# Raw residual rows with their reciprocal root in the gathers of an expert layer, and an earlier request for the tenth weight piece

## The chip, the cores and the metric

The kernel runs on one core of a Trainium2 chip. The metric is the device time of one execution of the whole program in microseconds (us), the median of several runs.

## The reference

One inference step of a two-layer decoder, for a prompt of 256 tokens and 32 sample tokens (8 sequences of 4), 1024 wide, all in float32. Layer 0 is a gated DeltaNet mixer, layer 1 differential attention; each is followed by a mixture of experts, and it is this part that the change touches:

```python
h = h + hier_moe(rms_norm(h, norm_m[layer]), w_rg, b_rg, w_re, b_re, w_gate, w_up, w_down)

# rms_norm: x * rsqrt(mean(x*x) + EPS) * g
# hier_moe: softmax over 4 groups, the best group; softmax over its 8 experts, the best two
def expert_block(args):            # 32 experts, 1024 -> 512 -> 1024
    xblk, e = args
    hid = jax.nn.silu(xblk @ w_gate[e]) * (xblk @ w_up[e])
    return hid @ w_down[e]
```

Each token's output is the sum of its two experts' outputs, weighted by the gates. The root-mean-square factor of a token is one number for its row, so (r x) W = r (x W).

## The kernel before

The program runs five phases one after the other: `gdn_phase`, `moe_phase` for layer 0, `attn_phase`, `moe_phase` for layer 1, `final_phase`. Each phase is one block with an instruction stream for each engine, and semaphores order them by hand. SP issues the loads and stores.

**Expert weights.** All 32 experts' weights pass through SBUF once in a layer: 96 pieces of 2 MiB (gate, up and down of each expert). They go round through ten slots (`SLOT_COUNT`, `slots`). A group is two experts, so six pieces, and there are 16 groups, 0 to 15 (`LAST`). Pieces 0 to 8 are requested before the phase, or at its start (4 and 5 in layer 1). Piece 9 goes to the tenth slot (L2082). From piece 10 on a piece is requested when the one ten before it has been read: `load` (L2085) works in halves of 1 MiB and waits for `half_used` and `used`, `load_whole` (L2097) waits for `used`; TensorE raises both in `stage` and `products`. Everything goes through SP's one queue in order.

**Routing.** The phase opens with the squares of the residual rows on ACT (L2187), whose full output goes into the tenth slot as scrap; the root (L2189) and its reciprocal `rstd` (L2263, DVE); TensorE's transposes of the residual (L2481) and the router's product (L2491). ACT then writes the normalised rows `xn` into the tenth slot, in the order that makes each 128-column tile contiguous (L2193), and SP stores them to `xn_dram` (L2077). POOL clears the unused 96 partitions of the third token tile of `xn`, in two memsets (L2149, L2151). A chain of small operations on DVE (L2269 to L2308) works out each token's experts and rank and ends in `sel0`, a 0/1 matrix that picks group 0's rows (L2308). Dummy products (L2502) fill TensorE meanwhile.

**Group 0** takes its rows from SBUF: 48 products of `xn` with `sel0` (L2625) give the transposed rows in `ps_x`; `gx_T` is raised at their end. SP waits for that before it asks for piece 9, since the piece overwrites `xn`.

**The other groups** gather 128 rows from `xn_dram` by an indirect DMA on POOL (L2167). Indices out of range are left out, so about a quarter of the rows move. The gather of group n+1 waits for the transposes of group n's rows (`gx_T`), and TensorE transposes what it brought (`rows_T`, L2520). DVE and ACT copy that out with the norm's gain (L2375, L2203).

**Order on TensorE in a group g:** the selection's transposes of group g-1 (L2575), gate (L2539), three sums of group g-1 (L2582), up (L2539), a fourth sum, the transposes of the hidden rows (L2548), the fifth sum (L2585), the transposes of group g+1's gathered rows (L2520), down (L2566). ACT applies SiLU to gate (L2209), DVE multiplies by up (`hidden`, L2381) and copies the transposes out (L2386).

## Time and profile before

| | us |
|---|---|
| three timed runs | 1522.5, 1524.02, 1524.5 |
| median | 1524.02 |
| the profiled execution | 1519.33 |
| its span | 1517.4 |
| expert phase, layer 0: first gate product to last | 366.9 to 799.0 (gate and up) |
| expert phase, layer 1: the same | 1056.0 to 1488.5 |

| engine | busy us | share of the span |
|---|---|---|
| PE (TensorE) | 1470.7 | 97% |
| DVE | 634.6 | 42% |
| ACT | 285.0 | 19% |
| POOL | 73.0 | 5% |

The page's span begins with the program's first work, and all positions below are microseconds from there. The profiled execution is one run more and is shorter than the three timed ones. PE's ends are modelled, and its products follow each other in a pipeline; a busy PE may still be waiting for a moment between two rows. The granted clock of TensorE is full (1.00, 2.4 GHz) in both expert phases.

### The profile page before, as it was taken

To read this page: it belongs to the slowest core of one execution; us is meant where nothing else is said; L and a number is where in the kernel's file an instruction comes from. 1 tells how busy PE (TensorE), PEld (TensorE's weight loads), DVE (VectorE), ACT (ScalarE), POOL (GpSimd) and SP (SyncE) were. 2 spreads that over 40 slices of the span, in tenths; PEclk is the share of its full clock that TensorE was granted. 3 is DMA by queue.
4 is the path that set the end of the run, shared out by engine and by line. 5 is a ranking of instruction groups with operands and counts; after the bars stand their busy time and mean duration, and the time that the engine had idled before them with its cause. 6 is when DMAs were issued, how large, how long until landed. Compare 5 with 4: busy or idle time off the path is not lost. (4 is left out here: it accounts for less than half of the span.)

```text
span 1517.4 us, 20326 instructions
## 1 busy us (share of the span) xinstructions
PE 1470.7 (97%) x7727; PEld 738.4 (49%) x7727; DVE 634.6 (42%) x1657; ACT 285.0 (19%) x746; POOL 73.0 (5%) x123
## 2 busy tenths in 40 slices
PE   9999999999999999999999998899999999999995
PEld 8787878667333333333334445657333333333331
DVE  3666566445323323224244235735232322433324
ACT  2424244214110101001001004523010100110101
POOL 0101010001000000000000000001000000000000
PEclk9999999999999999999999999999999999999998
DMA  7432324467999999999999036785999999999993
GB/s 232 137 116 75 116 78 143 187 230 308 417 430 431 428 429 433 430 428 426 426 427 368 19 126 257 268 343 204 412 429 431 430 429 431 431 430 426 427 426 157
DMA packets 101504, 484.54 MB, mean 319 GB/s; under 512 B 16410, under 2 KB 51134, under 8 KB 67634
## 3 DMA queue, kind: packets, MB, share of 16 engines
q1 hardware_dynamic: 96818, 478.90, 78.0%
q0 software_dynamic: 4320, 4.42, 0.8%
q8 instruction: 54, 0.88, 0.2%
q14 instruction: 24, 0.20, 0.0%
q10 hardware_dynamic: 288, 0.14, 0.0%
HBM read 483.77 MB, written 10.97 MB: 326 GB/s over the span
## 5 line engine op out<-in xcount | busy, mean ns | idle before, releaser
L2539 PE MATMUL moe_ps_gate<-slots,moe_xrT 128*64 128x512 f32 x1024 | 228.1, 596 | 8.5 <-DMA slots<-in_w_gate_e_dram 8.5
L2539 PE MATMUL moe_ps_up<-slots,moe_xrT 128*64 128x512 f32 x1024 | 226.8, 595 | 0.0
L2566 PE MATMUL moe_ps_y<-slots,router_inputs 128*64 128x512 f32 x960 | 212.6, 595 | 0.0
L2412 DVE TENSOR_TENSOR resid<-resid,moe_ps_x 128x512 f32<-128x512 f32 x60 | 41.3, 688 | 252.7 <-PE moe_ps_x L2582 252.7
L2539 PEld LDWEIGHTS moe_ps_up<-slots,moe_xrT 128*64 128x64 f32 x1024 | 71.2, 137 | 150.9 <-issue 138.7
L2539 PEld LDWEIGHTS moe_ps_gate<-slots,moe_xrT 128*64 128x64 f32 x1024 | 72.2, 137 | 137.9 <-issue 136.7
L966 PE MATMUL gdn_bank<-gdn_xT,slots 128*128 128x288 f32 x512 | 136.3, 410 | 0.7 <-ACT slots L485 0.7
L2566 PEld LDWEIGHTS moe_ps_y<-slots,router_inputs 128*64 128x64 f32 x960 | 66.3, 137 | 124.9 <-issue 124.6
L2203 ACT ACTIVATE moe_xrT<-moe_ps_x,router_inputs 128x128 f32<-128x128 f32 x128 | 36.5, 367 | 379.1 <-PE moe_ps_x L2520 363.5
L966 PEld LDWEIGHTS gdn_bank<-gdn_xT,slots 128*128 128x128 f32 x512 | 92.6, 190 | 22.8 <-issue 1.1
L2381 DVE TENSOR_TENSOR router_inputs<-router_inputs,moe_ps_up 128x512 f32<-128x512 f32 x32 | 22.0, 688 | 195.0 <-PE moe_ps_up L2539 195.0
L2209 ACT ACTIVATE router_inputs<-moe_ps_gate 128x512 f32<-128x512 f32 x32 | 19.1, 597 | 220.9 <-PE moe_ps_gate L2539 220.9
L2582 PE MATMUL moe_ps_x<-moe_y_sb,router_inputs 128*128 128x512 f32 x120 | 59.5, 618 | 0.0
L2219 ACT COPY moe_y_sb<-moe_ps_y 128x512 f32<-128x512 f32 x32 | 18.7, 585 | 193.6 <-PE moe_ps_y L2566 176.6
L2404 DVE COPY moe_y_sb<-moe_ps_y 128x512 f32<-128x512 f32 x30 | 20.7, 692 | 81.3 <-PE moe_ps_y L2566 81.3
L2167 POOL DMA_INDIRECT moe_xrT<-xn_rows,moe_rows_in x30 | 30.9, 1029 | 471.9 <-PE moe_ps_x L2520 470.0
L2396 DVE TENSOR_SCALAR moe_place<-consts,moe_lpos,moe_gcur 128x128 f32<-128x128 f32 x192 | 52.1, 345 | 1.2
L2416 DVE TENSOR_TENSOR resid<-resid,moe_ps_up 32x256 f32<-32x256 f32 x112 | 46.2, 413 | 2.6
L1730 PE MATMUL at_bank<-slots,at_XK 128*128 128x512 f32 x96 | 42.0, 596 | 0.0
L1730 PE MATMUL at_pair<-slots,at_XK 128*128 128x512 f32 x96 | 41.8, 593 | 0.0
L709 DVE SCALAR_TENSOR_TENSOR slots<-slots,gdn_cw 128x312 f32<-128x312 f32 x72 | 39.2, 545 | 2.5
L2582 PEld LDWEIGHTS moe_ps_x<-moe_y_sb,router_inputs 128*128 128x128 f32 x120 | 20.3, 189 | 38.7 <-issue 38.7
(509 smaller groups left out, 1817.9 us busy)
## 6 DMA issues: line engine op xcount, KB each, us to landing
slots<-in_w_gate_e_dram SPq DMA_DIRECT2D x40, 2048.0 KB, 23.0
slots<-in_w_up_e_dram SPq DMA_DIRECT2D x40, 2048.0 KB, 22.8
slots<-in_w_down_e_dram SPq DMA_DIRECT2D x40, 2048.0 KB, 25.8
slots<-in_w_gate_e_dram SPq DMA_DIRECT2D x48, 1024.0 KB, 26.2
slots<-in_w_up_e_dram SPq DMA_DIRECT2D x48, 1024.0 KB, 26.6
slots<-in_w_down_e_dram SPq DMA_DIRECT2D x48, 1024.0 KB, 26.0
slots<-in_w_in_a_dram SPq DMA_DIRECT2D x16, 1024.0 KB, 5.8
slots<-in_w_kv_dram SPq DMA_DIRECT2D x4, 2048.0 KB, 20.6
```

Of the source, the lines that this page charges most:

```text
L709: ins = V.scalar_tensor_tensor(acc[:, a, j, 0:ACC_COLS], src, cw[:, a, j, tap:tap + 1], acc[:, a, j, 0:ACC_COLS], ALU.mult, ALU.add)
L966: last = T.matmul(PB[i % 2][:, 0:T_ALL], w4[:, j, k, 128 * a:128 * a + 128], xT[:, k, :], start=(k == 0), stop=(k == KT - 1))
L1730: last = T.matmul(bank[:, :], XK[:, 0 if j < 2 else 1, k, at[t]], wslot[3 * half + j][:, k, :], start=(k == 0), stop=(k == KT - 1))
L2167: pool.indirect_dma_start(xg, None, xn_dram[:, :], bass.IndirectOffsetOnAxis(rows_in[:, :], 0), bounds_check=T_ALL - 1, oob_is_err=False). ...
L2203: last = A.activation(xgT[:, k, :], ps_x[:, 1, k - 4, :], ACT.Copy, scale=norm_T[:, k:k + 1])
L2381: V.tensor_tensor(hid, hid, ps_up[:], ALU.mult).then_inc(s["hidden"], 1)
L2396: last = V.tensor_scalar(place[:, k, t, :], m["lanes"][:, :], where[:, k, t:t + 1], gcur[:, k, t:t + 1], ALU.is_equal, ALU.mult)
L2412: V.tensor_tensor(half, half, banks[i][:, :], ALU.add).then_inc(s["summed"], 1)
L2416: V.tensor_tensor(part, part, banks[i][32 * q:32 * q + 32, 0:256], ALU.add).then_inc(s["summed"], 1)
L2539: last = T.matmul(ps[64 * e:64 * e + 64, :], xgT[:, k, 64 * e:64 * e + 64], slots[:, slot[2 * n + e], 512 * k:512 * k + 512], start=(k == ...
L2566: last = T.matmul(ps_y[64 * e:64 * e + 64, h, :], hidT[:, k, 64 * e:64 * e + 64], slots[:, slot[4 + e], 1024 * k + 512 * h:1024 * k + 512 ...
L2582: last = T.matmul(banks[i][:, :], selT[:, at[t]], y_sb[:, 512 * h:512 * h + 512], start=True, stop=True)
```

## The change

- ACT no longer writes normalised rows, and POOL's two memsets go. SP stores the residual rows as they are, first thing in the phase, and a row in DRAM is 1025 words long: `rstd` is stored into the last one, by three stores of one word a partition, once it is there.
- Piece 9 is requested right after the stores of the raw rows (and pieces 4 and 5 in layer 1), with no wait.
- Group 0's product takes the residual as its operand, and `sel0` carries `rstd` instead of 1.
- The gathers bring 1025 words a row. POOL then waits for the hidden rows of the group before and copies the last word to `rcur`. SiLU of the later groups has `rcur` as its scale, and DVE's product multiplies by it as well.
- The squares' scrap output goes to `y_sb`, one after the other; `low` and `rcur` get memory of their own, and `obf` moves into `y_sb`.
- The gathered rows stay in the order of the residual, so their transposes read with a stride of 8 words.

```diff
@@ sync
+            for t in range(NT):
+                sp.dma_start(xn_dram[128 * t:128 * t + rows[t], 0:D_MODEL], resid[0:rows[t], t, :]).then_inc(s["xn_stored"], 16)
             if layer:
                 m["prefetch"](sp, layer, (4, 5))
+            m["prefetch"](sp, layer, (9,))
+            sp.wait_ge(s["inverse"], 1)
             for t in range(NT):
-                sp.wait_ge(s["normed"], t + 1)
-                sp.dma_start(xn_dram[128 * t:128 * t + rows[t], :], xn[0:rows[t], t, :]).then_inc(s["xn_stored"], 16)
+                sp.dma_start(xn_dram[128 * t:128 * t + rows[t], D_MODEL:D_MODEL + 1], rstd[0:rows[t], t:t + 1], allow_slow_non_contiguous=True).then_inc(s["xn_stored"], 16)
             if layer == 0:
                 m["attn_inputs"](sp)
-            sp.wait_ge(s["xn_stored"], 16 * NT)
-            sp.wait_ge(s["gx_T"], 1)
-            m["prefetch"](sp, layer, (9,))
+            sp.wait_ge(s["xn_stored"], 16 * 2 * NT)
@@ gpsimd
             pool.wait_ge(s["folded"], 1)
-            P.memset(xn[32:64, 2, :], 0.0).then_inc(s["tail_cleared"], 1)
-            pool.wait_ge(s["tail_cleared"], 1)
-            P.memset(xn[64:128, 2, :], 0.0).then_inc(s["tail_cleared"], 1)
-            pool.wait_ge(s["tail_cleared"], 2)
             pool.wait_ge(s["logits_made"], NT)
-            P.memset(xg, 0.0).then_inc(s["cleared"], 1)
+            P.memset(xg_row, 0.0).then_inc(s["cleared"], 1)
             pool.wait_ge(s["cleared"], 1)
-            pool.wait_ge(s["xn_stored"], 16 * NT)
+            pool.wait_ge(s["xn_stored"], 16 * 2 * NT)
             pool.wait_ge(s["table_ready"], 1)
             def gather(n, row):
-                if not isinstance(n, int) or n > 1:
-                    pool.wait_ge(s["gathered"], n * 16 - 16)
                 P.tensor_copy(rows_in[:, :], row).then_inc(s["in_copied"], 1)
                 pool.wait_ge(s["in_copied"], n)
                 pool.wait_ge(s["gx_T"], n)
                 pool.sem_inc(s["waits_held"], 1)
-                pool.indirect_dma_start(xg, None, xn_dram[:, :], bass.IndirectOffsetOnAxis(rows_in[:, :], 0),
+                pool.indirect_dma_start(xg_row, None, xn_dram[:, :], bass.IndirectOffsetOnAxis(rows_in[:, :], 0),
                                         bounds_check=T_ALL - 1, oob_is_err=False).then_inc(s["gathered"], 16)
+                pool.wait_ge(s["gathered"], n * 16)
+                pool.wait_ge(s["hidden"], n)
+                pool.sem_inc(s["waits_held"], 1)
+                P.tensor_copy(rcur[:, :], xg_row[:, D_MODEL:D_MODEL + 1]).then_inc(s["r_kept"], 1)
@@ scalar
             for t in range(NT):
                 r = rows[t]
-                A.activation(xn[0:r, t, :], resid[0:r, t, :], ACT.Square, accum_out=ss[0:r, t:t + 1]).then_inc(s["squares"], 1)
+                if t:
+                    act.wait_ge(s["squares"], t)
+                A.activation(y_sb[0:r, :], resid[0:r, t, :], ACT.Square, accum_out=ss[0:r, t:t + 1]).then_inc(s["squares"], 1)
-            act.wait_ge(s["inverse"], 1)
-            for t in range(NT):
-                r = rows[t]
-                A.activation(by_tile(xn[0:r, t, :]), strided(resid[0:r, t, :]), ACT.Copy, scale=rstd[0:r, t:t + 1]).then_inc(s["normed"], 1)
@@ silu
-                A.activation(hid, ps_gate[:], ACT.Silu).then_inc(s["silued"], 1)
+                if isinstance(g, int) and g == 0:
+                    A.activation(hid, ps_gate[:], ACT.Silu).then_inc(s["silued"], 1)
+                else:
+                    act.wait_ge(s["r_kept"], g)
+                    A.activation(hid, ps_gate[:], ACT.Silu, scale=rcur[:, 0:1]).then_inc(s["silued"], 1)
@@ vector
-                    last = V.tensor_scalar(sel0[:, t, SLOTS * e:SLOTS * e + SLOTS], low, pos0[:, t, e:e + 1], None, ALU.is_equal)
+                    last = V.tensor_scalar(sel0[:, t, SLOTS * e:SLOTS * e + SLOTS], low[:, :], pos0[:, t, e:e + 1], rstd[:, t:t + 1], ALU.is_equal, ALU.mult)
@@ hidden
-                V.tensor_tensor(hid, hid, ps_up[:], ALU.mult).then_inc(s["hidden"], 1)
+                if isinstance(g, int) and g == 0:
+                    V.tensor_tensor(hid, hid, ps_up[:], ALU.mult).then_inc(s["hidden"], 1)
+                else:
+                    V.scalar_tensor_tensor(hid, hid, rcur[:, 0:1], ps_up[:], ALU.mult, ALU.mult).then_inc(s["hidden"], 1)
@@ tensor
-            xgv = by_tile(xg)
+            xgv = strided(xg)
-            pe.wait_ge(s["normed"], NT)
-            pe.wait_ge(s["tail_cleared"], 2)
             pe.wait_ge(s["sel0_made"], 1)
             for k in range(KT):
                 for t in range(NT):
-                    last = T.matmul(ps_x[:, k // 4, k % 4, :], by_tile(xn[:, t, :])[:, k, :], sel0[:, t, :], start=(t == 0), stop=(t == NT - 1))
+                    last = T.matmul(ps_x[:, k // 4, k % 4, :], strided(resid[0:rows[t], t, :])[:, k, :], sel0[0:rows[t], t, :], start=(t == 0), stop=(t == NT - 1))
@@ decoder_step
-    m["xn_dram"] = nc.dram_tensor("xn_rows", (T_ALL, D_MODEL), F32, kind="Internal").ap()
+    m["xn_dram"] = nc.dram_tensor("xn_rows", (T_ALL, D_MODEL + 1), F32, kind="Internal").ap()
```

## Rows read from the trace of the kernel before

**Rows 1.** The page: busy us (share of the span) x instructions of each engine

```profile
PE   1470.7 (97%) x7727; PEld 738.4 (49%) x7727; DVE 634.6 (42%) x1657; ACT 285.0 (19%) x746; POOL 73.0 (5%) x123
```

**Rows 2.** TensorE's timeline, layer 0, groups 12 to 15: start, us, engine line operation [idle before]

```profile
693.89 7.09 PE L2539 MATMUL moe_ps_gate<-slots,moe_xrT 128*64 128x512 f32 x32
...
721.39 3.65 PE L2539 MATMUL moe_ps_gate<-slots,moe_xrT 128*64 128x512 f32 x16
...
784.76 3.65 PE L2539 MATMUL moe_ps_gate<-slots,moe_xrT 128*64 128x512 f32 x16 [1.21 <-DMA slots<-in_w_gate_e_dram]
```

**Rows 3.** One stretch of layer 0: length, PE busy (x), granted clock, DMA share, GB/s

```profile
382.00:784.00 402.00, 398.66 (x1845) 1.00 1.01 428
```

**Rows 4.** TensorE's timeline, layer 1, gates of groups 13 and 15

```profile
1410.52 3.65 PE L2539 MATMUL moe_ps_gate<-slots,moe_xrT 128*64 128x512 f32 x16
...
1474.20 3.65 PE L2539 MATMUL moe_ps_gate<-slots,moe_xrT 128*64 128x512 f32 x16 [1.22 <-DMA slots<-in_w_gate_e_dram]
```

**Rows 5.** SP's timeline, both layers: when the DMAs are issued, and how long issuing took

```profile
365.68 0.81 SPq L2837 DMA_DIRECT2D slots<-in_w_up_e_dram  x2
370.59 4.26 SPq L2094 DMA_DIRECT2D slots<-in_w_down_e_dram  x4
381.06 0.89 SPq L2103 DMA_DIRECT2D slots<-in_w_gate_e_dram  x2
...
1032.83 2.00 SPq L2837 DMA_DIRECT2D slots<-in_w_down_e_dram  x4
...
1059.71 4.25 SPq L2094 DMA_DIRECT2D slots<-in_w_down_e_dram  x4
```

**Rows 6.** Stretches around piece 9 in layer 0, columns as in rows 3

```profile
366.50:368.00 1.50, 1.50 (x10) 1.00 1.00 197
368.00:370.60 2.60, 2.60 (x14) 1.00 0.95 400
...
372.40:381.00 8.60, 8.60 (x42) 1.00 1.00 406
```

**Rows 7.** The timeline of the routing, layer 0, ACT, DVE, PE and POOL

```profile
349.00 6.27 ACT L2193 ACTIVATE moe_last_slot<-resid,moe_rstd 128x1024 f32<-128x1024 f32 x3 [0.32 <-DVE moe_rstd L2263]
...
351.83 0.57 DVE L2269 SCALAR_TENSOR_TENSOR moe_logits<-moe_ps_hid,moe_rstd,router_inputs 128x36 f32<-128x36 f32 x3 [2.87 <-PE moe_ps_hid L2491]
...
360.00 5.60 PE L2625 MATMUL moe_ps_x<-moe_y_sb,moe_last_slot 128*128 128x128 f32 x48 [0.67 <-DVE moe_y_sb L2308]
...
368.54 1.19 POOL L2167 DMA_INDIRECT moe_xrT<-xn_rows,moe_rows_in  x1 [0.99 <-POOL moe_rows_in L2163]
```

**Rows 8.** DVE, four lines: count, duration ns min/median/max, first and last start us; forms

```profile
L2316 DVE TENSOR_SCALAR moe_place<-consts,moe_lpos x12: 279/282/288, 361.1 to 1051.2; 128x128 f32<-128x128 f32 x12
L2396 DVE TENSOR_SCALAR moe_place<-consts,moe_lpos,moe_gcur x192: 327/343/543, 384.8 to 1485.3; 128x128 f32<-128x128 f32 x192
L2771 DVE SCALAR_TENSOR_TENSOR resid<-resid,fin_ss,fin_norm x3: 1268/1277/1283, 1510.9 to 1513.3; 128x1024 f32<-128x1024 f32 x2, 32x1024 f32<-32x1024 f32 x1
L1700 DVE TENSOR_TENSOR at_q<-at_q,at_o_ss x2: 1219/1222/1226, 996.8 to 997.9; 128x1024 f32<-128x1024 f32 x2
```

**Rows 9.** Timeline of weight loads: eight strided (layer 0's start), eight contiguous (layer 1)

```profile
343.69 0.97 PEld L2481 LDWEIGHTS moe_ps_x<-consts,resid 128*128 128x128 f32 x8 [1.50 <-issue]
...
1071.89 0.92 PEld L2520 LDWEIGHTS moe_ps_x<-consts,moe_xrT 128*128 128x128 f32 x8
```

**Rows 10.** The timeline around the hidden rows of group 5, and POOL's gather after it

```profile
518.33 0.69 DVE L2381 TENSOR_TENSOR router_inputs<-router_inputs,moe_ps_up 128x512 f32<-128x512 f32 x1 [6.34 <-PE moe_ps_up L2539]
519.07 0.56 PEld L2548 LDWEIGHTS moe_ps_hid<-consts,router_inputs 128*128 128x128 f32 x4 [0.56 <-DVE router_inputs L2381]
522.25 1.02 POOL L2167 DMA_INDIRECT moe_xrT<-xn_rows,moe_rows_in  x1 [17.13 <-PE moe_ps_x L2520]
```

**Rows 11.** The page's queue 0 (gathers): packets, MB, share; landing of `xn_rows` (stores, gathers)

```profile
q0 software_dynamic: 4320, 4.42, 0.8%
DMA to landing us min/median/max: 4.3/10.0/12.2
```

More of the change, by code:

```diff
@@ L1953, in moe_phase @@
         slots = m["slots"]
-        sb("late_slots", [128, SLOT_COUNT - 7, SLOT_COLS])
-        xn = sb("last_slot", [128, SLOT_COLS])[:, 0:NT * D_MODEL].rearrange("p (t d) -> p t d", t=NT)
+        sb("late_slots", [128, SLOT_COUNT - 6, SLOT_COLS])
+        low = sb("low", [128, SLOTS])
+        rcur = sb("rcur", [128, 1])
         xrT = sb("xrT", [128, KT, T_ALL])
@@ L2008, in moe_phase @@
         sel0 = y_sb[:, 0:NT * 128].rearrange("p (t r) -> p t r", t=NT)
-        low = y_sb[:, NT * 128:NT * 128 + SLOTS]
         BELOW = -1024.0
         xr_flat = xrT[:].rearrange("p k r -> p (k r)")
-        xg = xr_flat[:, 0:1024]
-        xgT = xr_flat[:, 1024:2048].rearrange("p (k r) -> p k r", k=KT)
-        obf = xr_flat[0:1, 2048:2048 + 2 * OVER_GROUPS * N_EXPERTS].rearrange("p (b e) -> p b e", e=N_EXPERTS)
+        xg_row = xr_flat[:, 0:D_MODEL + 1]
+        xg = xr_flat[:, 0:D_MODEL]
+        xgT = xr_flat[:, 1032:2056].rearrange("p (k r) -> p k r", k=KT)
+        obf = y_sb[0:1, 768:768 + 2 * OVER_GROUPS * N_EXPERTS].rearrange("p (b e) -> p b e", e=N_EXPERTS)
         selT = w_router.rearrange("p k n -> p (k n)")[:, 0:T_ALL]
@@ L2039, in moe_phase @@
         s = {n: sem(n) for n in (
-            "squares ss_cleared tail_cleared roots inverse normed xn_stored xT_made xT_kept folded logits_made logits_kept gdiff gexped tdiff texped hots ranked "
+            "squares ss_cleared roots inverse xn_stored r_kept xT_made xT_kept folded logits_made logits_kept gdiff gexped tdiff texped hots ranked "
             "sel0_made first_T placed tabbed table_ready v cleared waits_held in_copied gathered gx_T gx0_kept gx1_kept gate_made up_made y_made "
@@ L2260, in _ @@
                     V.tensor_copy(xrT[:, 4 * j:4 * j + 4, at[t]], ps_xT[t][:, j, :, 0:rows[t]]).then_inc(s["xT_kept"], 1)
-            link(V.tensor_scalar(low, m["lanes"][:, 0:SLOTS], BELOW, None, ALU.add))
+            link(V.tensor_scalar(low[:, :], m["lanes"][:, 0:SLOTS], BELOW, None, ALU.add))
             dve.wait_ge(s["roots"], 1)
```

## The prediction

> **What bounds the kernel now.** I read the page first. TensorE is busy 97% of the span [rows 1], and over 402 us of an expert phase the DMA share is 1.01 beside it [rows 3]. Two resources both full do not say which one sets the time, so the next view is TensorE's timeline in the first expert phase. A group of two experts is gate, up and down, with the sums of the group before between them. Group 12's gate begins at 693.89 and group 13's at 721.39, 27.50 us later, with no idle time before any step [rows 2]. So here TensorE is the bound, although the DMA share says 1.01. But a group wants 6 pieces of 2.097 MB, 12.58 MB, and the stretch of [rows 3] moves 428 GB/s. That is 29.4 us a group. Each group puts the stream 1.9 us further behind, and the ten slots are the reserve that it eats. It is eaten in group 13: waits for a slot's landing appear in the gates of groups 13, 14 and 15 only, and the second half of group 15's gate begins at 784.76 [rows 2]. At 27.50 us a group it would have begun at 721.39 + 55.00 + 3.51 = 779.90 (3.51 us is half of a gate: the row's 7.09 less the 0.07 us by which its modelled end runs into the next step, halved). The stream costs layer 0 4.9 us. Layer 1 repeats it: 1474.20 instead of 1410.52 + 58.51 = 1469.03, 5.2 us [rows 4]. So 10.0 us of the span are lost to the stream. The rest of the expert phases is TensorE's, and the end of each is set by when the last gate pieces land, the moment M.
>
> Two consequences carry the rest. Work added to TensorE or on the chain of groups 1 to 14 is free up to 4.9 us in a layer. And M moves only if the stream's own start or its bytes move.
>
> **The change part by part.**
>
> *The tenth slot's piece asked for first.* Now it is issued at 365.68, after the transposed gather products of group 0; the change issues it right after the raw rows are stored, some 20 us sooner. This looks like 2.097 MB / 428 GB/s = 4.9 us off the stream, but the stream behind it does not wait for it: piece 10 may be issued only when the first half of group 0's gate has been read, at 370.59 [rows 5], and nothing of the change moves that forward. The question is how much of piece 9 is still in the queue then. [Rows 6] has it: 197 x 1.5 + 400 x 2.6 = 1335 KB are through by 370.6, the 762 KB left take 1.8 us at 428 GB/s, to 372.4. After the change pieces 10 and 11 find an idle queue, and an idle queue is slow at first: piece 9, issued at 365.68, moved nothing until about 366.5 and then 197 GB/s for 1.5 us, 0.8 us less of transfer than at 428. So they begin at 370.6 + 0.8 = 371.4, 1.0 us sooner, and lose 0.8 us again to the slow start. From the other side there is a cap: the pair after them is issued at 381.06, when group 0's up has been read [rows 5], and starts no sooner than 381.9. In the kernel before, what stands in front of it is 2.097 + 4.194 MB of pieces and a gather of 0.147 MB (4.42 MB in 30 [rows 11]), from 366.5: 1335 + 770 + 3492 KB are through by 381.0, and the 0.84 MB left at 428 GB/s end at 383.0. The stream cannot gain more than 1.1 us there, and 0 is as likely. I take 0.2 us for each layer, ends 0 and 1.1, and the same in layer 1, whose piece 10 is issued at 1059.71 [rows 5].
>
> *Normalised rows gone.* Three ACT copies end at 355.27 and the two POOL memsets lie beside the router's transposes. What sets gate 0 is the routing chain on DVE: logits at 351.83, sel0 last, and TensorE's idle 0.67 us before it starts group 0's product at 360.00 waits for sel0, with ACT done 4.7 us before [rows 7]. Worth 0. The cover is DVE's chain; ACT would need 4.7 us more to show. The squares now wait for each other, two semaphore waits of about 0.1 us: rstd is ready by 349.00, where its copies begin, and is first wanted at 351.83 [rows 7], so 0 as well.
>
> *sel0 times rstd.* Six TENSOR_SCALAR of 128x64 get a second operation with a second pointer. With 128 columns the form with one is 282 ns and the form with two 343 ns [rows 8]; half the columns, half the difference, 30 ns each. 6 x 0.03 = +0.2 us on the chain before gate 0, ends 0 and 6 x 0.061 = 0.4. It moves gate 0, so also the release at 370.59, so M: exposed.
>
> *Raw rows as TensorE's weights.* Both the group 0 product and the transposes of gathered rows now read with a stride of 8. The phase's first transposes read resid that way: their eight weight loads take 0.97 us, eight contiguous ones 0.92 [rows 9]. The 0.05 us may be the last load's alone, or 0.006 us of each. For a group's transposes that is 0.05 us either way, hidden in the 4.9. For the 48 loads of the group 0 product the ends are -0.2 (the third token tile has 32 rows now, not 128) and +0.3; I take 0.
>
> *Hidden and the factor.* SCALAR_TENSOR_TENSOR with rcur instead of TENSOR_TENSOR. With 1024 columns they take 1277 and 1222 ns [rows 8]. The 55 ns belong to the instruction or to its columns, of which hidden has half: +28 to +55, ends 0 and 55. I take 40. This is on a chain: hidden starts at 518.33 and TensorE's next transposes load at 519.07, right behind it [rows 10]. At 0.055 us it is 0.8 us over 14 groups, inside the 4.9. Only group 15, behind M, pays: +0.04 in a layer. SiLU's scale pointer on ACT: 0.
>
> *POOL's extra wait and copy.* rcur is copied after the hidden of the group before. Behind it on POOL stand the index copy and the next gather. The hidden ends at 519.02; two one-word copies with their semaphores, put at 0.8 us, and the 0.99 us that stood between index copy and gather once [rows 7] give 520.8, and the gather of today starts at 522.25, after the transposes [rows 10]. 0, with 1.4 us of margin, and the gather lands 10.0 us later [rows 11], while its rows are wanted by the next group's transposes, 27.50 us after these: some 15 us of slack stand behind the margin.
>
> *Stores.* The raw rows go out at the phase's start. Three stores of 4 bytes a partition follow piece 9 in SP's queue, and SP's wait for them stands before piece 10; layer 0's attention inputs are issued between. In layer 1 the queue, issued from 1032.83 on [rows 5], is then 1.18 + 4.19 + 2.10 MB, 17.4 us, with 1.6 us for its slow start to 1052; I add up to 4 us for the column, from the 4.3 us that the fastest store took to land [rows 11]: 1056. SP wants it at 1059.7 and POOL at 1056.5, and POOL's first gather is wanted 15 us later. 0; it would cost from 3.7 us more on.
>
> *Gathers of 4100 bytes.* A gather's share is 0.8% of 16 engines over 1517.4 us, 12.1 us for 30 gathers, 0.40 us each [rows 11]. Of these 14 lie in each bounded stretch, and there DMA time is exposed. If the time goes with the bytes it is +0.006 us in a layer, 0, which I take; no row bounds the upper end well, so half as much again is rival (b).
>
> By a rule of the Trainium skill, "DMA: Bandwidth & Descriptors", section "How a descriptor splits into AXI transactions", a run that does not begin on a 256-byte boundary fetches from the boundary below. Rows of 4100 bytes lose the alignment: 17 or 18 pieces instead of 16, an estimate of 6 to 12% more gather time, up to 0.05 x 14 = 0.7 us in a layer. By it the sum would be about +1.4 us higher; the trace of before holds no unaligned gather.
>
> **The sum**, for each layer: -0.2 (stream) + 0.2 (sel0) + 0.04 (last hidden) = about 0, for two layers +0.1 us. On the profiled execution, 1519.33 us with 1517.4 span, that is 1519.4; the median of the three timed runs, 1524.02, lies 4.7 us above it, and the change is set on that: 1524.1 us. Bounds for a layer, gathers apart: -1.1 (stream) - 0.2 (weights) = -1.3, and +0.4 + 0.3 + 0.055 = +0.8. For both layers -2.6 to +1.6, and with 0.7 us of scatter (the three runs lie 2 us apart) 1520.8 to 1526.4.
>
> **Rivals.**
> (a) *The stream gains the whole piece.* If M follows the bytes queued behind it and not the releases, each layer wins all its 4.9 and 5.2 us, less 0.2 for sel0: -9.5, 1514.5 us. For: the DMA line is 1.00 or more from 366.5 on [rows 3, 6]. Against: the issues of [rows 5] follow TensorE's reads. 10%.
> (b) *Slower through the gathers.* The odd row length, 1025 words, makes the queue move each row in more or slower packets. If a gather takes half as long again, +0.20 x 14 = 2.8 us in a layer, +5.6, 1529.7 us; TensorE cannot hide it, since M is the stream's. It decides from +0.11 us a gather, which makes 3 us. For: no row here has such a length, and and queue 0 is at 0.045 us for a packet of 1023 bytes in the mean, where the big ones pay 16 x 1023 / 428000 = 0.038 [rows 3, 11], so smaller ones are dearer. Against: 4 bytes in 4096. 15%.
> (c) *It does not do what it says*: piece 9 stays behind the column stores' wait or the stores of raw rows hold it. Then the stream gains 0 and the time is 1524.5, inside the forecast.
>
> **How the numbers follow.** 3.0 us, 0.2%, is about what a measurement can tell from no change. Forecast with (c): 72%, all within. (a) 10%. (b) 15%, four fifths of it above 3 us. The other 3%: an unseen stall. Faster 0.11, same 0.74, slower 0.15. The forecast's own range holds 72%; to reach 80% it is carried toward (b), the likelier side: 1520.8 to 1529.8.
>
> **What would show it.** In the profile after: piece 9 issued near 346 and 1035 and gone before 364 and 1053; pieces 10 and 11 issued 0 to 0.4 us later than now against gate 0; periods of 27.50 to 27.56 us; waits for slots still only in gates 13 to 15, 4 to 5 us in a layer; hidden 690 to 745 ns. It is wrong if those waits are gone (a), if they grow while the gather's share of the queue grows (b), or if TensorE idles in front of the transposes of gathered rows.

## The result, and the profile after

The changed kernel takes 1550.62 us (median, 1549.49 to 1554.35) where the kernel before takes 1523.26: a ratio of 1.0185, 95% interval 1.0164 to 1.0206. The forecast was no change: 1524.1 us, between 1520.8 and 1529.8. The execution profiled took 1549.49 us with a span of 1547.4, 30.0 more than the 1517.4 before; the medians lie 27.4 apart, since the execution profiled before was faster than its median.

The first view to open is TensorE's timeline where group 0 of layer 0 starts (start, us, engine, line, operation, idle before). Of the changed kernel:

```profile
360.53 16.23 PE L2628 MATMUL moe_ps_x<-moe_y_sb,resid 128*128 128x128 f32 x48 [0.94 <-DVE moe_y_sb L2310]
376.68 2.90 PE L2635 MATMUL moe_ps_tab<-moe_entry,moe_place 128*128 128x32 f32 x12
379.51 9.45 PE L2544 MATMUL moe_ps_gate<-slots,moe_xrT 128*64 128x512 f32 x32
```

The same view of the kernel before, the two steps behind the product of [rows 7]:

```profile
365.43 1.53 PE L2632 MATMUL moe_ps_tab<-moe_entry,moe_place 128*128 128x32 f32 x12
366.89 7.09 PE L2539 MATMUL moe_ps_gate<-slots,moe_xrT 128*64 128x512 f32 x32
```

Group 0's product takes 16.23 us, not 5.60; the table product 2.90, not 1.53; gate 0 9.45, not 7.09. The instructions are as many as before and their shapes nearly the same, so two questions follow: what slows the product's instructions, and what slows two steps whose code is unchanged. Layer 1 of the changed kernel repeats it:

```profile
1065.12 16.01 PE L2628 MATMUL moe_ps_x<-moe_y_sb,resid 128*128 128x128 f32 x48 [0.94 <-DVE moe_y_sb L2310]
1081.07 2.90 PE L2635 MATMUL moe_ps_tab<-moe_entry,moe_place 128*128 128x32 f32 x12
1083.90 8.83 PE L2544 MATMUL moe_ps_gate<-slots,moe_xrT 128*64 128x512 f32 x32
```

The second question is answered by stretches of the changed kernel (length; busy us of PE, PEld, DVE, ACT, POOL; granted clock, DMA share, GB/s):

```profile
359.00:360.00 1.00, 0.59 (x5) 0.43 (x4) 0.96 (x6) 0.00 (x0) 0.00 (x0) 1.00 1.18 348
360.00:361.00 1.00, 0.47 (x2) 0.48 (x3) 0.93 (x6) 0.00 (x0) 0.00 (x0) 0.71 0.91 328
...
370.00:384.00 14.00, 14.00 (x44) 9.23 (x46) 3.86 (x20) 2.42 (x5) 1.39 (x2) 0.50 0.04 10
384.00:385.00 1.00, 1.00 (x8) 0.28 (x6) 0.97 (x7) 0.00 (x0) 0.00 (x0) 0.84 0.10 29
```

The granted clock falls to 0.50, 1.2 GHz, 0.1 us before the product starts, and is back at 1.00, 2.4 GHz, after 384. In layer 1 it falls 1.8 us after the product's start. In the kernel before it is 1.00 over this whole stretch. The table product and gate 0's first half run at the low level: +1.4 and +2.4 us. In 370 to 384 the DMA share is 0.04: the stream stands still, for want of a released slot. SyncE's issues of the changed kernel, piece 9 and then piece 10 of layer 0, and piece 10 of layer 1, say how long:

```profile
345.29 0.89 SPq L2840 DMA_DIRECT2D slots<-in_w_up_e_dram  x2
...
385.63 4.19 SPq L2096 DMA_DIRECT2D slots<-in_w_down_e_dram  x4
...
1089.40 4.18 SPq L2096 DMA_DIRECT2D slots<-in_w_down_e_dram  x4
```

Piece 9 goes 20.39 us earlier than in [rows 5], and piece 10 goes 15.04 us later. The last gate pieces (the prediction's M) land later by about as much, in TensorE's timeline of the changed kernel, against [rows 2, 4]:

```profile
800.65 3.65 PE L2544 MATMUL moe_ps_gate<-slots,moe_xrT 128*64 128x512 f32 x16 [1.23 <-DMA slots<-in_w_gate_e_dram]
...
1504.10 3.65 PE L2544 MATMUL moe_ps_gate<-slots,moe_xrT 128*64 128x512 f32 x16 [1.41 <-DMA slots<-in_w_gate_e_dram]
```

M moves by 15.89 us in layer 0 and 29.90 in all. The budget of the 15.04 to piece 10: 0.53 until the product starts (0.28 came before the phase, 0.25 from the selection), 10.72 product, 1.37 table product, 2.42 gate 0's first half. So the loss lies ahead of the middle of gate 0. The 0.85 us by which M moves more than piece 10 in layer 0 lie inside what this distance scatters from trace to trace, as the table below shows.

The weight loads of the product, changed kernel, timeline of PEld:

```profile
360.52 1.03 PEld L2628 LDWEIGHTS moe_ps_x<-moe_y_sb,resid 128*128 128x128 f32 x4 [1.05 <-DVE moe_y_sb L2310]
361.78 0.55 PEld L2628 LDWEIGHTS moe_ps_x<-moe_y_sb,resid 32*128 32x128 f32 x2 [0.22 <-issue]
362.55 1.03 PEld L2628 LDWEIGHTS moe_ps_x<-moe_y_sb,resid 128*128 128x128 f32 x4 [0.22 <-issue]
```

Four loads of 128 rows take 1.03 us, then comes a pause of 0.22, two loads of 32 rows in 0.55, and a pause of 0.22 again: 2.02 us for each of the eight column tiles, where 5.60 / 8 is 0.70 before. So three things differ at once: the step of the columns (8 words), the height of the third token tile (32 rows, not 128), and the clock.

### The profile page after: what moved, and what is told of

It is laid out like the page before. It is cut to its first block and busy times, and to the rows that moved or that the text cites. A ratio compares the mean times of both kernels' runs of the same rounds, so it can differ in the third digit from the quotient of the medians.

```text
span 1547.4 us, 20410 instructions
## 1 busy us (share of the span) xinstructions
PE 1502.0 (97%) x7727; PEld 760.2 (49%) x7727; DVE 636.7 (41%) x1657; ACT 275.6 (18%) x740; POOL 74.7 (5%) x149
## 5 line engine op out<-in xcount | busy, mean ns | idle before, releaser
L2544 PE MATMUL moe_ps_gate<-slots,moe_xrT 128*64 128x512 f32 x1024 | 231.8, 604 | 6.7 <-DMA slots<-in_w_gate_e_dram 6.7
L2201 ACT ACTIVATE moe_xrT<-moe_ps_x,router_inputs 128x128 f32<-128x128 f32 x128 | 36.5, 367 | 401.6 <-PE moe_ps_x L2525 364.5
L2386 DVE SCALAR_TENSOR_TENSOR router_inputs<-router_inputs,moe_rcur,moe_ps_up 128x512 f32<-128x512 f32 x30 | 22.4, 747 | 183.4 <-PE moe_ps_up L2544 183.4
L2211 ACT ACTIVATE router_inputs<-moe_ps_gate,moe_rcur 128x512 f32<-128x512 f32 x30 | 20.6, 687 | 206.7 <-PE moe_ps_gate L2544 206.7
L2168 POOL COPY moe_rcur<-moe_xrT 128x1 f32<-128x1 f32 x30 | 5.4, 181 | 689.6 <-DVE router_inputs L2386 661.2
```

The lines of the kernel that those rows point to most:

```text
L2201: last = A.activation(xgT[:, k, :], ps_x[:, 1, k - 4, :], ACT.Copy, scale=norm_T[:, k:k + 1])
L2386: V.scalar_tensor_tensor(hid, hid, rcur[:, 0:1], ps_up[:], ALU.mult, ALU.mult).then_inc(s["hidden"], 1)
L2544: last = T.matmul(ps[64 * e:64 * e + 64, :], xgT[:, k, 64 * e:64 * e + 64], slots[:, slot[2 * n + e], 512 * k:512 * k + 512], start=(k == ...
```

## The experiments

The kernel before ran beside every group of runs, with medians of 1522.2 to 1523.9 us. Each trace shows one execution of its kernel.

**The height alone restored.** The changed kernel, padded:

```
+P.memset(resid[32:64, 2, :], 0.0); P.memset(resid[64:128, 2, :], 0.0)
-T.matmul(..., strided(resid[0:rows[t], t, :])[:, k, :], sel0[0:rows[t], t, :])
+T.matmul(..., strided(resid[:, t, :])[:, k, :], sel0[:, t, :])
```

> The changed kernel, with the third token tile of group 0's product at 128 rows again (the residual's unused rows are cleared by two POOL memsets, so all six weight loads of a column tile have one height). Reads stay strided by 8, everything else of the change stays. Theory height (weights of 32 rows between weights of 128 rows cost at every switch, and the emptier TensorE loses its clock): the product takes 5.6 to 6.0 us instead of 16.2, the granted clock stays 1.00, and the time is that of the kernel before within 3 us. Rival stride (the strided two-pass float32 weights are what is slow): the product stays above 11 us and the time near 1550. Rival gap (the clock falls because TensorE idles 0.94 us before the product instead of 0.67, the product only runs at that clock): product 11 to 12 us, clock 0.50 in it, the two steps behind it longer too, time about 1542.

1536.91 us, ratio 1.0094 (1.0077 to 1.0110). Its TensorE timeline:

```profile
362.01 11.70 PE L2633 MATMUL moe_ps_x<-moe_y_sb,resid 128*128 128x128 f32 x48 [1.03 <-DVE moe_y_sb L2314]
373.54 1.53 PE L2640 MATMUL moe_ps_tab<-moe_entry,moe_place 128*128 128x32 f32 x12
375.01 7.09 PE L2548 MATMUL moe_ps_gate<-slots,moe_xrT 128*64 128x512 f32 x32
```

11.70 us is the price of the step with the height gone. The clock is at 0.50 for 3.4 us only (364.5 to 367.9), so the table product and gate 0 are as before. Half of the loss goes.

**The height alone, in the kernel before.** The product reads 32 rows of the third tile, contiguous and normalised:

```
-by_tile(xn[:, t, :])[:, k, :], sel0[:, t, :]
+by_tile(xn[0:rows[t], t, :])[:, k, :], sel0[0:rows[t], t, :]
```

> The kernel before, with one thing of the change: group 0's product reads 32 rows of the third token tile instead of 128. Reads are contiguous, the idle gap ahead of it is the 0.67 us of before. Height: the product goes from 5.6 us to 8 at full clock or to 16 if the clock falls too, and the time rises by 5 us (full clock) to 29 us (half clock), both layers together. Stride and gap: no change, 1523.

1534.78 us, 1.0086 (1.0057 to 1.0114). Reading fewer rows makes the product slower, 8.48 us at a granted clock of 1.00, and the clock falls behind it, where gate 0 starts (in layer 1 already in the table product, and gate 0 takes 9.96 us). The four runs lie between 1530.90 and 1539.46 us, with a mean granted clock of 0.992 in the two short ones and of 0.986 and 0.989 in the two long ones, so a run's length here goes with how long the clock stays low. Timeline, then stretches:

```profile
361.03 8.48 PE L2625 MATMUL moe_ps_x<-moe_y_sb,moe_last_slot 128*128 128x128 f32 x48 [0.67 <-DVE moe_y_sb L2308]
371.00 8.78 PE L2539 MATMUL moe_ps_gate<-slots,moe_xrT 128*64 128x512 f32 x32
```

```profile
360.00:371.70 11.70, 11.03 (x67) 8.53 (x68) 5.67 (x29) 2.14 (x5) 0.20 (x1) 0.99 0.12 23
371.70:374.60 2.90, 2.90 (x10) 0.88 (x8) 2.56 (x12) 0.29 (x1) 1.19 (x1) 0.50 1.01 410
```

2.88 us over 16 changes of height are 0.18 us a change.

**The step alone, in the kernel before.** The eight column tiles are read with the step of 8 out of the normalised rows, so group 0's columns come in another order:

```
-by_tile(xn[:, t, :])[:, k, :]
+strided(xn[:, t, :])[:, k, :]
```

> The kernel before, with group 0's product reading the normalised rows with a stride of 8 words (group 0's columns then come in another order than its weights expect: this part of the computation is changed). All heights are 128, the gap is that of before. Stride: product above 11 us and the time 10 to 27 us longer. Height and gap: no change, 5.6 us and 1523.

1535.60 us, 1.0076 (1.0059 to 1.0093). The product takes 11.68 us. It is the step and not what is read (raw or normalised, resid or the slot): 6.1 us more for 48 loads, 0.24 us from load to load where it was 0.113. The clock was at 0.50 for 3.4 us here too, but that adds nothing that shows. Stretches of 1 us (length, PE busy and products, granted clock, DMA share, GB/s) hold 6 products at either level:

```profile
365.00:366.00 1.00, 1.00 (x6) 0.50 0.00 0
...
369.00:370.00 1.00, 1.00 (x6) 1.00 0.06 16
```

The pace is the same at 1.00 and at 0.50. In layer 1 the clock fell a second time, as gate 0 started, and gate 0 took 8.69 us.

**The idle gap filled.** In the changed kernel TensorE idles 0.94 us ahead of the product; four products to an unused place fill it.

```
+keep_busy(4)
 pe.wait_ge(s["sel0_made"], 1)
```

> The changed kernel, with four more dummy products (about 0.9 us) on TensorE between the count product and the wait for sel0, so that the idle gap ahead of group 0's product is below 0.2 us. Nothing else is changed. Gap: the clock stays 1.00 through the product, the product takes 6 to 9 us and the time falls to between 1523 and 1532. Height, in the form that the product's own sparse pattern loses the clock: the clock falls inside the product, as in layer 1 of the changed kernel (1.8 us after its start), and 11 us or more are still lost in each layer, time 1544 to 1551.

1550.76 us, 1.0186 (1.0169 to 1.0203): no gain. Stretches, then the product:

```profile
359.00:365.00 6.00, 6.00 (x31) 5.39 (x31) 5.42 (x28) 0.00 (x0) 0.00 (x0) 1.00 1.02 296
365.00:385.00 20.00, 20.00 (x62) 13.51 (x64) 5.35 (x25) 2.43 (x5) 1.39 (x2) 0.50 0.11 32
```

```profile
361.13 15.80 PE L2629 MATMUL moe_ps_x<-moe_y_sb,resid 128*128 128x128 f32 x48
```

The clock falls with no gap ahead. It falls at 365.1, 4.7 us later and 4.0 us into the product, and the product is 0.4 us shorter. So the low clock is a small part of the 16.23.

**Everything else of the change, without the product.** Raw rows of 1025 words, the factor's copy, SiLU and hidden with the factor stay; group 0's product reads normalised, padded rows from the tenth slot again, with 1 instead of the root in `sel0`, and piece 9 waits for it.

```
+A.activation(by_tile(xn[0:r, t, :]), strided(resid[0:r, t, :]), ACT.Copy, scale=rstd[0:r, t:t + 1])
-T.matmul(..., strided(resid[0:rows[t], t, :])[:, k, :], sel0[0:rows[t], t, :])
+T.matmul(..., by_tile(xn[:, t, :])[:, k, :], sel0[:, t, :])
+sp.wait_ge(s["gx_T"], 1)
 m["prefetch"](sp, layer, (9,))
```

> All of the change except two parts: group 0's product reads normalised, padded, contiguous rows from the tenth slot, as before the change, and piece 9 is therefore asked for after that product again. What stays of the change: raw rows of 1025 words stored and gathered, the copy of the factor on POOL, SiLU with a scale from a pointer, the three-input hidden product, the squares written in a chain, the selection's free-standing low row. Theory (all that was lost hangs on the product's weights): ratio to before 0.998 to 1.002, that is 1520 to 1526 us, the product at 5.6 us and the granted clock at 1.00 all through. Rival (the factor's steps in the 14 groups, with +90 ns of SiLU and +59 ns of hidden each, are not hidden): 28 groups by 0.15 us are 4.2 us, so a ratio of 1.003 or more.

1522.50 us, 1.0000 (0.9990 to 1.0010). The first row is a group of VectorE's, with the mean of one in ns, the other two are gates 27.63 us apart:

```profile
L2396 DVE SCALAR_TENSOR_TENSOR router_inputs<-router_inputs,moe_rcur,moe_ps_up 128x512 f32<-128x512 f32 x14 | 10.5, 748 | 88.8 <-PE moe_ps_up L2554 88.8
```

```profile
420.78 7.09 PE L2554 MATMUL moe_ps_gate<-slots,moe_xrT 128*64 128x512 f32 x32
448.41 7.09 PE L2554 MATMUL moe_ps_gate<-slots,moe_xrT 128*64 128x512 f32 x32
```

Hidden is dearer and each group 0.13 us longer than the 27.50 of [rows 2], and the kernel is no slower within 1.5 us: the slack ahead of M takes it.

**The early request alone.** The padded run again, with piece 9 asked for after the product.

```
-m["prefetch"](sp, layer, (9,))
 sp.wait_ge(s["inverse"], 1)
 ...
+sp.wait_ge(s["gx_T"], 1)
+m["prefetch"](sp, layer, (9,))
```

> The changed kernel with its third token tile padded to 128 rows (as the earlier run of that kind, 1536.9 us), and with piece 9 asked for only after group 0's product and the stores. It prices the early request alone, against that earlier run. My theory: the early request is worth 0.2 to 1.1 us a layer, so this run gives 1537.3 to 1539 us (ratio to before 1.0093 to 1.0105). Rival (the stream is what bounds the group loop and all of the 24 us by which piece 9 goes earlier counts, up to its transfer of some 4.9 us a layer): 1542 to 1547 us (1.012 to 1.0155). A third case: nothing, 1536.9.

1535.24 us, 1.0077 (1.0065 to 1.0090), against 1.0094 with the early request. Later is not slower. Times that lie 2 us apart in different groups of runs do not price it finely; M less the issue of piece 10 does. The rows of this run, SyncE and then TensorE:

```profile
379.17 4.24 SPq L2097 DMA_DIRECT2D slots<-in_w_down_e_dram  x4
```

```profile
793.05 3.65 PE L2549 MATMUL moe_ps_gate<-slots,moe_xrT 128*64 128x512 f32 x16 [1.22 <-DMA slots<-in_w_gate_e_dram]
```

| kernel | piece 9 | M less issue of piece 10, layer 0 / 1 |
|---|---|---|
| before | late | 414.17 / 414.49 |
| changed | early | 415.02 / 414.70 |
| padded | early | 414.70 / 414.68 |
| padded, asked late | late | 413.88 / 414.68 |
| rest of the change | late | 414.02 / 414.38 |

M follows the release of piece 10 by 414 to 415 us, whatever piece 9 does. Over all 14 traces, those of the runs below included, the distance lies between 413.9 and 415.8, with a mean of 414.8 for the seven early ones and 414.6 for the seven late ones. The request 20 us ahead buys nothing that stands out of this scatter of about 1 us.

**The disputed price by itself.** In the kernel before, the 26 filling products of the routing are exchanged for 28 with chosen weights; the moving operand has one column fewer in each set, so that the profile keeps them apart.

```
-keep_busy(26)
+for j, (step, tall, short) in enumerate(((1, 128, 128), (2, 128, 128), (4, 128, 128), (8, 128, 128), (1, 128, 32), (1, 128, 64), (1, 32, 32))):
+    for i in range(4):
+        r = tall if i % 2 == 0 else short
+        wide = resid[0:r, 0, 0:128 * step].rearrange("p (c s) -> p s c", s=step)[:, 0, :]
+        T.matmul(ps_gate[:, 0:128 - j], wide, ones[0:r, 0:128 - j], start=True, stop=True)
```

> The kernel before, with the 26 filling products of 128 columns that keep TensorE busy while the routing is worked out exchanged for 28 products that write to the same unused place: four each with weights from resid at a step of 1, 2, 4 and 8 words, then four each at a step of 1 word with the weights' rows alternating 128 and 32, alternating 128 and 64, and all of 32 rows. It measures the disputed price by itself; the output stays the same. Theory: two weight loads a product, at 0.11 us from load to load at a step of 1 and 0.24 us at a step of 8, so 0.9 and 1.9 us for the four; alternating 128 and 32 rows costs 0.18 us a switch (about 0.5 us over the four), while 32 rows alone cost nothing over 128. Rivals: the price at a step of 2 is already the full one (a matter of contiguity), or it grows with the step (a matter of the bytes between columns); or the steps cost nothing here and the 11.7 us of the strided product came from something else in its place.

Groups of TensorE in layer 0 at a granted clock of 1.00, by form (busy us, mean ns; 128 columns are step 1, 127 step 2, 126 step 4, 125 step 8, 124 heights 128 and 32 in turn, 123 heights 128 and 64, 122 all of 32):

```profile
L2509 PE MATMUL moe_ps_gate<-consts,resid 128*128 128x125 f32 x8 | 2.1, 402 | 0.0
L2509 PE MATMUL moe_ps_gate<-consts,resid 128*128 128x126 f32 x8 | 2.0, 397 | 0.0
...
L2509 PE MATMUL moe_ps_gate<-consts,resid 128*128 128x128 f32 x8 | 1.2, 288 | 0.0
L2509 PE MATMUL moe_ps_gate<-consts,resid 32*128 32x122 f32 x8 | 1.1, 283 | 0.0
L2509 PE MATMUL moe_ps_gate<-consts,resid 128*128 128x127 f32 x8 | 1.1, 282 | 0.0
L2509 PE MATMUL moe_ps_gate<-consts,resid 128*128 128x123 f32 x4 | 1.0, 324 | 0.0
L2509 PE MATMUL moe_ps_gate<-consts,resid 64*128 64x123 f32 x4 | 1.0, 321 | 0.0
L2509 PE MATMUL moe_ps_gate<-consts,resid 32*128 32x124 f32 x4 | 1.0, 320 | 0.0
L2509 PE MATMUL moe_ps_gate<-consts,resid 128*128 128x124 f32 x4 | 0.9, 300 | 0.0
```

Steps of 1 and 2 words cost the same (1.2 and 1.1 us for four products); 4 and 8 words nearly double it (2.0 and 2.1). So neither rival holds as it was put: the price is not due at once, and does not grow on from 4 words. All of 32 rows costs what 128 cost; 128 and 32 in turn take 1.9 us together, 0.2 us a change, and 128 and 64 take 2.0. The Trainium skill, "SBUF — State Buffer", section "Door 1: The DMA port swizzle", says that reads run at full rate with at least two hits in each 16-byte line; two words and four fall on the two sides of that, as measured. The same passage puts a step of 4 float32 among the free ones; for the weights of an ordinary product this run shows the contrary, 2.0 us against 1.2.

The clock fell behind this filling as well, and the untouched product of the kernel before ran partly at 0.50:

```profile
364.16 8.29 PE L2629 MATMUL moe_ps_x<-moe_y_sb,moe_last_slot 128*128 128x128 f32 x48 [0.42 <-DVE moe_y_sb L2308]
```

It took 8.29 us instead of 5.60. The low level held until 369.8, for 5.6 us of it; stretches of 1 us hold 6 or 7 products there and 11 at 1.00. So the low clock nearly doubles the time of a product with contiguous weights, to about the pace that the strided one has at either level. The one run took 1537.49 us.

**The operands exchanged.** The changed kernel whole, but the selection is the weights and the raw rows stream past it, contiguous; eight transposes then make the layout.

```
+for h in range(2):
+    for t in range(NT):
+        T.matmul(ps_y[:, h, :], sel0[0:rows[t], t, :], resid[0:rows[t], t, 512 * h:512 * h + 512], start=(t == 0), stop=(t == NT - 1))
+A.copy(xg[:, 512 * h:512 * h + 512], ps_y[:, h, :])
+T.transpose(ps_x[:, k // 4, k % 4, :], xgv[:, k, :], ident[:, :])
```

> The changed kernel whole, early request for piece 9 included, but with the two operands of group 0's product exchanged: the selection (contiguous, 128 columns) is the weights and the raw residual rows stream past it in two halves of 512 columns, six products in all; ScalarE copies the two halves from PSUM, and eight transposes of the kind that the other 14 groups use bring them into the layout of the gates. Theory (the loss is the price of residual rows as weights of an ordinary product, and transposes with the same step are cheap): six products of 0.87 us (from 16 of 64 columns of weights, side by side in pairs, in the 7.09 us of a gate) are 5.2 us, the second copy 0.6 to 0.7, the transposes 1.15, so 7.1 us in place of 5.6 before and 16.2 after; with nothing else late, 1.5 to 2.5 us a layer over before, 1526 to 1529 us in all (ratio 1.002 to 1.0035), and the granted clock at 1.00. Rival (the early request or the raw rows themselves cost something that the padded run hid): over 1535 us. A third: the early request earns what the exchange costs, 1522 to 1525.

1532.32 us, 1.0058 (1.0043 to 1.0073). 18 us of the loss are gone, short of the 22 or more expected. Layer 0:

```profile
360.73 7.70 PE L2632 MATMUL moe_ps_y<-resid,moe_y_sb 128*128 128x512 f32 x12 [0.94 <-DVE moe_y_sb L2314]
369.11 1.15 PE L2636 MATMUL moe_ps_x<-consts,moe_xrT 128*128 128x128 f32 x8 [0.68 <-ACT moe_xrT L2226]
...
371.97 10.01 PE L2548 MATMUL moe_ps_gate<-slots,moe_xrT 128*64 128x512 f32 x32
```

The transposes read with the same step of 8 and take 1.15 us, so they don't pay for it. The clock was at 0.50 from 360.9 to 364.2 and from 371.1 to 377.9. In layer 1, with the clock at 1.00, the six products take 6.00 us, more than the 5.2 expected, and the clock falls only ahead of gate 0 (8.43 us). One of the six runs took 1526.71 us, at a mean granted clock of 0.993 against 0.989 to 0.992 in the others.

**Filling inside the strided product.** Two filling products ahead of each column tile of the changed kernel.

```
 for k in range(KT):
+    keep_busy(2)
```

> The changed kernel with two filling products of 128 columns (contiguous weights, written to an unused place) ahead of each of the eight column tiles of group 0's product. Theory (the granted clock falls because little passes through TensorE while it loads strided weights, and the fall costs about 5 us a layer: 1.6 in the product, 1.4 in the table product, 2.4 in gate 0): with the clock held at 1.00, the product's own part takes 14.6 us, the filling 16 by 0.24 us are 3.8 us more, the table product 1.53 and gate 0 7.09: 18.4 + 1.53 + 7.09 = 27.0 us against the changed kernel's 28.6, so 1.5 us a layer faster than it, some 1547.5 us (ratio to before 1.0165). Rival (the clock falls whatever stands between, or the heights' alternation costs by the number of switches, which the filling raises): 16.2 + 3.8 us or more for the product, with gate 0 at 9.4, so 1558 us or more (1.0225).

1562.57 us, 1.0264 (1.0250 to 1.0277): the theory falls. The clock falls at 364 in spite of the filling, and the filling is paid in full: 12.0 us over the changed kernel are 6.0 a layer, more than the 3.8 expected, since each filling of four loads takes 1.0 us start to start at the low level. But the first column tile ran before that, at 1.00, the later ones at 0.50:

```profile
362.13 1.78 PE L2629 MATMUL moe_ps_x<-moe_y_sb,resid 128*128 128x128 f32 x6
...
370.49 1.91 PE L2629 MATMUL moe_ps_x<-moe_y_sb,resid 128*128 128x128 f32 x6
```

Eight of 1.78 are 14.2 us, an estimate of what the product takes at full clock with step and heights together (each tile ends in filling here, not in the next tile). The two single runs add up to 5.60 + 6.1 + 2.9 = 14.6.

**The exchanged operands, gaps filled.** Four products ahead of the selection, three ahead of the transposes.

```
+keep_busy(4)
 pe.wait_ge(s["sel0_made"], 1)
 ...
+keep_busy(3)
 pe.wait_ge(s["rows0_kept"], 2)
```

> The run with exchanged operands (selection as weights, 1532.3 us), with its two idle gaps on TensorE filled by products to an unused place: four of 128 columns (0.94 us) ahead of the wait for the selection, three (0.7 us) between the six products and the transposes, which wait for ScalarE's second copy. Theory (with little strided weight loading left, the gaps of 0.94 and 0.68 us are what the granted clock falls after): the clock stays at 1.00, the six products take 6.0 us in both layers, the table product 1.53 and gate 0 7.09, which is 5.0 us less in layer 0 and 1.6 less in layer 1 than without the filling: 1525.5 to 1526.5 us, ratio to before 1.0015 to 1.0025. Rival (the fall comes from something else, as it did when the gap ahead of the strided product was filled): the clock still falls, and the time stays at 1530 to 1533 us.

1526.50 us, 1.0025 (1.0014 to 1.0036), as worked out; the twelve runs lie between 1523.94 and 1531.20.

```profile
361.01 6.00 PE L2633 MATMUL moe_ps_y<-resid,moe_y_sb 128*128 128x512 f32 x12
366.94 0.94 PE L2511 MATMUL moe_ps_gate<-consts 128*128 128x128 f32 x6
367.71 1.14 PE L2638 MATMUL moe_ps_x<-consts,moe_xrT 128*128 128x128 f32 x8
368.69 1.53 PE L2645 MATMUL moe_ps_tab<-moe_entry,moe_place 128*128 128x32 f32 x12
370.15 7.09 PE L2548 MATMUL moe_ps_gate<-slots,moe_xrT 128*64 128x512 f32 x32
```

With no gap and no strided product the clock stays at 1.00 in both layers of the execution profiled (1525.92 us).

**The table product in the second gap.** It stands between the six products and the transposes.

```
-keep_busy(3)
+pe.wait_ge(s["placed"], TOP_K)
+T.matmul(ps_tab[:, 0:2 * MAIN_GROUPS], place[0:rows[t], k, t, :], entry[0:rows[t], k, t].rearrange("p a c -> p (a c)"), ...)
+last.then_inc(s["tabbed"], 1)
 pe.wait_ge(s["rows0_kept"], 2)
```

> The same exchanged operands with the same four filling products ahead of the wait for the selection, but the second gap is filled with work that is needed: the table product (1.53 us) stands between the six products and the transposes. Gate 0 then waits for the copies of the transposed rows (0.69 us on VectorE after the first four transposes) that the table product had covered. Theory: 6.0 + 1.53 + 0.6 + 0.7 to 0.9 for the copy, so gate 0 starts 8.9 us after the selection against 9.3 with the filling alone, and the table is ready 1.8 us earlier, which nobody waits for: 1525 to 1526 us if the clock holds. Rival: the new wait ahead of gate 0 is again a gap after which the clock falls, and gate 0 takes 8.4 us or more in place of 7.09 in each layer: 1528 us or more.

1530.53 us, 1.0054 (1.0039 to 1.0068): the rival. A gap of 0.41 us ahead of gate 0 took the place of the one filled. In the execution profiled (1526.86 us, the shortest of six) both layers had this gap; layer 0 kept its clock and layer 1 lost it, with gate 0 at 8.78 us.

**A gap alone.** The kernel before, with the selection multiplied by the root as in the change.

```
-..., low, pos0[:, t, e:e + 1], None, ALU.is_equal)
+..., low, pos0[:, t, e:e + 1], rstd[:, t:t + 1], ALU.is_equal, ALU.mult)
```

> The kernel before, with one edit: the six selection instructions multiply by the reciprocal root from a pointer as in the changed kernel, while the product still reads normalised rows (so group 0's tokens carry the factor twice, and their part of the output is changed). It prices the selection's second operation alone, and lengthens TensorE's idle gap ahead of the product from 0.67 to some 0.94 us with everything else as before. Theory A (a gap alone of 0.9 us is enough for the granted clock to fall): the clock drops to 0.50 near the product or gate 0 as it did with the exchanged operands, at 1.7 to 5 us a layer, so 1527 us or more (ratio 1.0025 or more). Theory B (it takes the gap and sparse loading together): the clock stays at 1.00, the product at 5.6 us, and the time rises by 2 by 0.25 us only, 1523.5 us (ratio 1.0003, at most 1.001).

1524.06 us, 1.0015 (1.0003 to 1.0027): theory B in its mechanism, with a ratio somewhat above the 1.001 that it allowed. The gap grew by 0.36 us, and in the execution profiled (1521.92 us, among the shortest of twelve) the product and the clock did not notice. The mean granted clock of the twelve runs is 0.991 to 0.996, that of the kernel before beside them 0.992 to 0.996, so nothing speaks for a fall in the others:

```profile
361.81 5.60 PE L2625 MATMUL moe_ps_x<-moe_y_sb,moe_last_slot 128*128 128x128 f32 x48 [1.03 <-DVE moe_y_sb L2308]
```

```profile
361.80:367.20 5.40, 5.39 (x48) 5.40 (x49) 4.09 (x19) 0.00 (x0) 0.00 (x0) 1.00 0.01 3
```

## Why the prediction was wrong, point by point

**The step that failed** is "Raw rows as TensorE's weights": "For the 48 loads of the group 0 product the ends are -0.2 (the third token tile has 32 rows now, not 128) and +0.3; I take 0." It measured +10.6 and +10.4 us in the two layers. Three errors stand in it.

- *The row did not carry the case.* [Rows 9] compares transposes, eight loads that stand 0.12 us apart with either step. The operation to be priced was an ordinary product, with two loads for each of its 24 products, 0.113 us apart. Both kinds load more slowly with the step (193 ns against 141 for a transpose, 336 against 192 in the product), but only the product's loads then follow each other more slowly. The two differ in operation and number of loads. The step costs 6.1 us a layer.
- *The lower rows were booked as a gain.* They were the -0.2 at the lower end, and no row stood behind it. The change of height between loads costs 0.18 us, 16 times: +2.9.
- *The clock was not in the sum.* It fell in each run whose product was strided or of two heights. In the changed kernel that is some 1.6 us of the product, 1.37 of the table product and 2.42 of gate 0 in layer 0 (1.7 in layer 1). Ahead of the prediction nothing asked whether TensorE keeps its level when its loads slow down. The kernel before has 26 filling products ahead of group 0's product, and [rows 6] show a clock of 1.00 behind it; no row told what a slower product would do to it.

Together with the 0.25 us of the selection and the 0.28 from ahead of the phase, these three (6.1, 2.9 and 1.6 + 1.37 + 2.42) make 14.9 of the 15.04 us by which piece 10 was late in layer 0. The 1.6 is what is left of 16.23 after 14.6.

**What held.** M moves only with the stream's start: the 15.04 us by which piece 10 was issued later arrived at M undiminished, and slack that hid 0.12 us a group (gates 27.62 us apart in the changed kernel, a little over the 27.56 forecast) hid none of it. *The early request*: 0.2 us taken, nothing measured within about 1 us; rival (a), 4.9 us, is refuted by the late request of the padded run. Of piece 10's release the prediction said that "nothing of the change moves that forward"; that the change could move it back, by 15.04 us, it did not ask. *Normalised rows gone*: 0, since the routing chain ends later. *sel0 times rstd*: 0.2 taken with ends 0 and 0.4; the gap grew from 0.67 to 0.94 (0.36 in the run of its own). *Hidden*: 747 ns against 688 in the groups of the changed kernel, +59 where the upper end was 55. *SiLU's pointer* was put at 0 and is 687 ns against 597. Both are hidden, as said. *POOL's wait and copy*: 0, as said; in the changed kernel's group 4 POOL still waited 2.62 us for TensorE's transposes before it issued the gather. *Gathers*, rival (b): on the changed kernel's page the line of queue 0 is the one of [rows 11] unchanged, and the run with all of them came out at 1.0000.

The rule of the Trainium skill, "DMA: Bandwidth & Descriptors", section "How a descriptor splits into AXI transactions", which the prediction weighed at up to 0.7 us a layer, is neither borne out nor excluded by that: twice 0.7 us lies just inside the interval of that run. (Its 18 pieces cannot occur, by an estimate from the same rule, with a row as one descriptor: one that starts on a multiple of 4 bytes ends at most 252 + 4100 = 17 x 256 bytes behind a boundary, so 17 pieces, and half of the 0.7 us.)

**The range** was closed by rows that shared the step but not the operation. In the trace of before a strided transpose's load takes 193 ns and a contiguous one's 141; what such a difference does to loads that come in pairs, 0.113 us apart, no row told. One more such distance for each of the 48 loads, 5.4 us a layer, was the upper end to write down. Even that would have left the result outside: the heights and the clock were not in it.

**Open.** What exactly makes the granted clock fall. A gap of 1.03 us ahead of a dense product did not do it; a strided product without a gap did; the exchanged product, with gaps and no strided weights, did too, and stopped when the gaps were filled; 0.41 us was followed by a fall in one layer and not in the other. The padded product, asked late, had a second fall ahead of gate 0 in layer 0 (8.62 us), which the padded one asked early did not have. Nor is it shown why transposes with the same step go free, why a step of 4 words costs and one of 2 does not, or why a change of height costs: these are measured, not explained. A contiguous copy of the raw rows beside the ten slots was not tried.

None of these versions beats the kernel before. The early request earns nothing, so freeing the tenth slot has no use here.

## What to carry to other kernels

Before an operand's layout is changed, find out which operand of TensorE it becomes: as weights of an ordinary float32 product, columns 4 or 8 words apart took twice the time from load to load here, and weights of alternating heights took longer than padded ones; in a transpose the step of 8 words cost nothing that shows. With the operands exchanged the same rows stream past contiguous and need no step (a moving operand with a step was not measured). Price such an edit by a row of the same operation, and if there is none, leave the range wide. And where a stream waits for a release, an earlier request in front of that release is worth nothing, while the time by which the release itself slips is paid in full, 15 us a layer here.

## What the runs showed of the hardware that was not expected

- Fewer rows in some of the weights made a product slower: 8.48 us with every third tile of 32 rows, 5.60 with all of 128, at the same clock.
- Columns 2 words apart are loaded like contiguous ones, 4 apart like 8 apart: 1.1, 2.0 and 2.1 us for four products.
- At a granted clock of 0.50 a strided product hardly slows (1.91 us a column tile against 1.78), while one of contiguous weights goes from 5.60 to 8.29 with the low level for two thirds of it: 6 or 7 products a microsecond there, 11 at 1.00.
- A pointer as SiLU's scale costs 90 ns on 128x512.
